# A hybrid decoder layer in one Trainium2 core: the short convolution's norm takes its power of 128x256 instead of 128x2

## The chip, the core and the metric

The kernel runs on one core of a Trainium2 chip. The metric is device time in microseconds. The median of three timed runs before the change is 1239.05 us (1238.25 to 1240.45). The engines of the core are named as in the profile: PE (TensorE, matmuls), PEld (its weight loads), DVE (VectorE), ACT (ScalarE), POOL (GpSimd), SP (SyncE, here the queue that issues the weight DMAs).

## The reference, cut to what matters

The layer is: RMSNorm, one input projection (`w_in`, 2048 to 6144), attention on 8 heads, a gated short convolution on the other 1024 columns, an output projection, cross-attention into 256 memory tokens, a SwiGLU FFN and a final RMSNorm, all for 256 tokens in float32. The change touches the norm of the convolution branch:

```
y_conv = b_gate * short_conv(c_gate * x_in, w_conv, b_conv)
y_conv = rms_norm(y_conv.reshape(bsz, s_len, CONV_GROUPS, HEAD_DIM), g_conv_out...)   # 8 groups of 128 columns
merged = jnp.concatenate([o_attn..., y_conv...], axis=-1);  return merged @ w_out
```

`rms_norm(x, g)` is `x * rsqrt(mean(x*x) + 1e-6) * g`, the mean here over the 128 columns of a group, for each token by itself.

## The kernel before, in words

All large products run over one stream of weights. A step `j` is one pair of 128-row weight tiles, 128x1024: a DMA of SP brings it into `raw`, ACT casts it to `whi` (L644), DVE forms the rest `wlo = raw - whi` (`split`, L937), and PE does 12 matmuls of 128x512 with it (`step`, L378 to L380: high by high, high by low, low by high, for two halves of the tokens). ACT and DVE run the cast and the split of step `j + 2` (`LEAD`) in their iteration `j`, and the ring has four places. There is no planner: the order on each engine is the order in the code, an iteration `j` after another, and semaphores hold an engine until its input is there. PE's step `j` waits for `lo_ready` (the split of step j).

The steps that matter here are 88 to 111. Steps 88 to 95 are the last group of the input projection (`G_X`), 96 to 103 the keys of the memory (`G_KX`), 104 to 111 the first group of the output projection (`G_OUT`). In iterations 94 to 101 ACT and DVE also prepare the memory's activations for steps 96 to 103 (`untransposed`, L680 on ACT, two instructions at L972 on DVE, signal `m_lo`). Steps 108 to 111 wait for `merged_conv`: step 111 for all eight blocks of the convolution.

The convolution is laid between the steps. It has 8 blocks `b` of 128 channels; block b starts at step s = 92 + 2b (`CONV_START`), and its channels lie on the partitions, its 256 tokens on the free axis. By iteration of each engine:

- s: PE transposes x and the gate into PSUM (L467), ACT forms two products of it (L778, L779), DVE adds the two other taps and the gate (`conv_taps`, L1089, L1092, L1094).
- s+1: ACT squares it into `csq` (L786).
- s+2: PE sums the squares over the partitions, 2 matmuls of 128x1 with `csq` as the weights (`conv_sums`, L475), so that the sums lie with tokens on the partitions, 128x2. DVE scales them and adds the epsilon (`conv_mean`, L1098). POOL takes the power -0.5 of 128x2 (L356).
- s+3: DVE writes the roots on two 128x128 diagonals, over `csq` (`conv_diagonal`, L1105).
- s+4: PE multiplies ones by these diagonals (`conv_spreading`, L482), so that each partition has the root of each token, and DVE scales y with it and the gain (`conv_scale`, L1112).
- s+5: ACT writes the high part (`conv_out`, L790), POOL the low part (L359, signal `merged_conv`).

POOL's order is: the product `u` of blocks 0 to 3 (L352, 128x1024), powers 0 and 1, the product of blocks 4 to 7 (L352 again), then low part 0, power 2, low part 1, power 3, and so on, so that the low part of b stands right behind the power of b + 1. On DVE, in one iteration, the order is `split`, `conv_taps`, `conv_mean`, `conv_diagonal`, `conv_scale`, `untransposed`.

Of the kernel before, what the change touches and what calls it, by code (L numbers as in the profile page):

```python
# [20 lines left out]
P = 128  # L21
# [72 lines left out]
def build(nc, stream, x, xT, mem, memT, params, pos, inv_freq, g_final, out):  # L94
# [4 lines left out]
    with ctx:  # L99
# [3 lines left out]
        def sb(name, shape, dt=f32, at=None):  # L103

            size = 4 * int(np.prod(shape[1:]))
            spot = place if at is None else at
            line = LINE if size >= LINE else 64
            where = -(-spot[0] // line) * line
            spot[0] = where + -(-size // 64) * 64
            return nc.alloc_sbuf_tensor_at(name, shape, dt, offset=where)  # L110
# [6 lines left out]
        def sem(name):  # L117
            return ctx.enter_context(nc.semaphore(name))
# [14 lines left out]
        rstd = sb("rstd", [P, 4, TT])  # L133
        vpe = sb("vpe", [P, 4, TT])
        part = sb("part", [P, TT, D // GC])
        cvar = sb("cvar", [P, CB, TT])
        crstd = sb("crstd", [P, CB, TT])
        fss = sb("fss", [P, TT])
        fvar = sb("fvar", [P, TT])
        frstd = sb("frstd", [P, TT])  # L140
# [23 lines left out]
        uT = sb("uT", [P, 2, 2 + SEQ], at=conv_at)  # L164
        cy = sb("cy", [P, 4, SEQ], at=conv_at)
        csq = sb("csq", [P, 4, SEQ], at=conv_at)
        place[0] = max(place[0], conv_at[0])
        assert place[0] <= nc.sbuf_usable_end, (place[0], nc.sbuf_usable_end)
        par_cols = G_KX * GC
# [68 lines left out]
        u_ready, conv_T, conv_u = sem("u_ready"), sem("conv_T"), sem("conv_u")  # L238
        conv_tap, conv_y, conv_sq = sem("conv_tap"), sem("conv_y"), sem("conv_sq")
        conv_ss, conv_var, conv_root = sem("conv_ss"), sem("conv_var"), sem("conv_root")  # L240
        conv_diag, conv_spread = sem("conv_diag"), sem("conv_spread")
        conv_norm, conv_hi, merged_conv = sem("conv_norm"), sem("conv_hi"), sem("merged_conv")
        pad_ready = sem("pad_ready")
        q2_T, q2T_ready = sem("q2_T"), [sem("q2T_by_act"), sem("q2T_by_dve")]
# [27 lines left out]
        def gain(col):  # L272
            return par[:, ds(col, 1)]
# [24 lines left out]
        @block.gpsimd  # L298
        def _(pool):
            pool.memset(ident[:], 0.0).then_inc(blank, 1)  # L300
            pool.memset(mask[:], 0.0).then_inc(blank, 1)
            pool.memset(ones[:], 1.0).then_inc(consts_ready, 1)
            pool.memset(mhalf[:], -0.5).then_inc(consts_ready, 1)
            pool.wait_ge(blank, 2)
            pool.affine_select(out=ident[:], in_=ident[:], compare_op=ALU.not_equal, fill=1.0, base=0,
                               pattern=[[-1, P]], channel_multiplier=1).then_inc(consts_ready, 1)
            for n in (0, 2):
                pool.affine_select(out=mask[:, n * P:(n + 1) * P], in_=mask[:, n * P:(n + 1) * P],
                                   compare_op=ALU.is_ge, fill=MASKED, base=0,
                                   pattern=[[-1, P]], channel_multiplier=1).then_inc(consts_ready, 1)  # L310

            def root(n):

                pool.wait_ge(var_ready, n + 1)
                nc.gpsimd.tensor_tensor(rstd[:, n, :], vpe[:, n, :], mhalf[:], ALU.pow).then_inc(rstd_ready, 1)

            def rope(h, parity):
                src = proj[:, :, ds(AW + h * (2 * HD), 2 * HD)].rearrange("p t (q f) -> p t q f", q=2)
                lo_half, hi_half = src[:, :, :, 0:HD // 2], src[:, :, :, HD // 2:HD]
                pool.wait_ge(rope_done, 2 * h)  # L320
                for n, (a, b) in enumerate(((lo_half, cos), (hi_half, sin), (hi_half, cos), (lo_half, sin))):
                    nc.gpsimd.tensor_tensor(rtmp[:, n], a, b[:], ALU.mult).then_inc(rope_products, 1)
                pool.wait_ge(rope_products, 4 * h + 4)
                dst = qkr[:, parity]
                nc.gpsimd.tensor_tensor(dst[:, :, :, 0:HD // 2], rtmp[:, 0], rtmp[:, 1], ALU.subtract).then_inc(rope_done, 1)
                nc.gpsimd.tensor_tensor(dst[:, :, :, HD // 2:HD], rtmp[:, 2], rtmp[:, 3], ALU.add).then_inc(rope_done, 1)

            def head_root(h):
                pool.wait_ge(o_var, h + 1)
                nc.gpsimd.tensor_tensor(orstd, ovar, mhalf[:], ALU.pow).then_inc(o_rstd, 1)  # L330

            pool.wait_ge(consts_ready, 2)
            root(0)
            root(1)
            pool.wait_ge(table_ready, 4)
            await_out(pool, G_QK)
            rope(0, 0)
            rope(1, 1)
            with pool.Fori(0, NH // 2 - 1) as i:
                for n in range(2):  # L340
                    h = i * 2 + n
                    head_root(h)

                    pool.wait_ge(qk_T, h + 1)
                    rope(h + 2, n)
            head_root(NH - 2)
            head_root(NH - 1)
            c0, x0 = (G_C - G_V) * GC, (G_X - G_V) * GC
            for n in range(2):
                await_out(pool, G_X + n)  # L350
                u = proj[:, :, x0 + n * GC:x0 + (n + 1) * GC]
                nc.gpsimd.tensor_tensor(u, proj[:, :, c0 + n * GC:c0 + (n + 1) * GC], u, ALU.mult).then_inc(u_ready, 1)  # L352
                for j in range((G_X + 1) * SPG, G_KX * SPG + 1) if n == 0 else range(G_KX * SPG + 1, G_XQ * SPG):
                    for b in conv_blocks(j, 2):
                        pool.wait_ge(conv_var, b + 1)
                        nc.gpsimd.tensor_tensor(crstd[:, b, :], cvar[:, b, :], mhalf[:], ALU.pow).then_inc(conv_root, 1)  # L356
                    for b in conv_blocks(j, 5):
                        pool.wait_ge(conv_hi, b + 1)
                        nc.gpsimd.tensor_tensor(alo[:, NH + b, :], cy[:, b % 4, :], ahi[:, NH + b, :].bitcast(f32),  # L359
                                                ALU.subtract).then_inc(merged_conv, 1)  # L360
            root(2)
            root(3)
            for t in range(TT):
                pool.wait_ge(fvar_ready, t + 1)
                nc.gpsimd.tensor_tensor(frstd[:, t:t + 1], fvar[:, t:t + 1], mhalf[:, 0:1], ALU.pow).then_inc(frstd_ready, 1)  # L365
# [3 lines left out]
        def _(pe):  # L369
# [101 lines left out]
            def conv_sums(b):  # L471

                pe.wait_ge(conv_sq, b + 1)
                for t in range(TT):
                    done = nc.tensor.matmul(ps[:, CONV_BANKS[b % 4], SEQ + t:SEQ + t + 1],  # L475
                                            lhsT=csq[:, b % 4, t * P:(t + 1) * P], rhs=ones[:, 0:1], start=True, stop=True)
                done.then_inc(conv_ss, 1)

            def conv_spreading(b):

                pe.wait_ge(conv_diag, b + 1)
                nc.tensor.matmul(ps[:, CONV_BANKS[b % 4], 0:SEQ], lhsT=ones[:], rhs=csq[:, b % 4, :],  # L482
                                 start=True, stop=True).then_inc(conv_spread, 1)

            def conv_beside(j):

                for b in conv_blocks(j, 4):
                    conv_spreading(b)
                for b in conv_blocks(j, 2):
                    conv_sums(b)  # L490
                for b in conv_blocks(j, 0):
                    conv_front(b)
# [141 lines left out]
        def _(act):  # L634
# [147 lines left out]
            def conv_square(b):  # L782
                act.wait_ge(conv_y, b + 1)
                if b >= 4:
                    act.wait_ge(conv_spread, b - 3)
                nc.scalar.activation(csq[:, b % 4, :], cy[:, b % 4, :], ACT.Square).then_inc(conv_sq, 1)  # L786

            def conv_out(b):
# [140 lines left out]
        def _(dve):  # L929
# [165 lines left out]

            def conv_mean(b):
                dve.wait_ge(conv_ss, b + 1)
                vec.tensor_scalar(cvar[:, b, :], ps[:, CONV_BANKS[b % 4], SEQ:SEQ + TT], 1.0 / HD, EPS,  # L1098
                                  ALU.mult, ALU.add).then_inc(conv_var, 1)

            def conv_diagonal(b):

                dve.wait_ge(conv_root, b + 1)
                for t in range(TT):
                    done = vec.tensor_scalar(csq[:, b % 4, t * P:(t + 1) * P], ident[:], crstd[:, b, t:t + 1], None, ALU.mult)  # L1105
                done.then_inc(conv_diag, 1)

            def conv_scale(b):

                y = cy[:, b % 4, :]  # L1110
                dve.wait_ge(conv_spread, b + 1)
                vec.scalar_tensor_tensor(y, y, gain(C_CONV + b), ps[:, CONV_BANKS[b % 4], 0:SEQ],  # L1112
                                         ALU.mult, ALU.mult).then_inc(conv_norm, 1)

            dve.wait_ge(scores_ready, NH)
# [15 lines left out]
            for j in range((G_X + 1) * SPG + 3, J_XO):  # L1131
# [5 lines left out]
                    conv_taps(b)  # L1137
                for b in conv_blocks(j, 2):
                    conv_mean(b)
                for b in conv_blocks(j, 3):  # L1140
                    conv_diagonal(b)
                for b in conv_blocks(j, 4):
                    conv_scale(b)
                u = j - (G_X + 1) * SPG - 6
# [158 lines left out]
```

## Time and profile before

| | before |
|---|---|
| median of 3 runs | 1239.05 us |
| profiled execution, its own time | 1238.83 us |
| its span (first to last instruction) | 1237.0 us |
| PE busy | 1220.4 us (99%) |
| DVE, ACT, POOL busy | 676.0, 593.5, 87.6 us |
| DMA | 234.36 MB, mean 189 GB/s |

A busy share says only that an engine had work in its pipeline. What a change is worth is read from the chain of waits and from the timeline of its stage: which instruction an engine was waiting for when it stood still. POOL is idle for most of the span, and DVE for nearly half of it.

### The profile page before, as it was taken

How to read it: one execution, taken by the hardware profiler on the slowest of the kernel's cores; microseconds unless marked ns; L12 is line 12 of the kernel's file. 1: busy time of each engine (PE TensorE's matmuls, PEld its weight loads, DVE VectorE, ACT ScalarE, POOL GpSimd, SP SyncE). 2: the span in 40 equal slices, each digit the busy share in tenths (PEclk: the TensorE clock that was granted, in tenths of full speed). 3: DMA queues.
4: the chain of work that ended last, by engine and by line, in shares of the span. 5: the costliest groups of instructions: out<-in, count | busy, mean ns of one | idle time of the engine just before them, and what ended most of it. 6: DMA issues, size and time to landing. Idle time of an engine off the chain costs nothing.

```text
span 1237.0 us, 16477 instructions
## 1 busy us (share of the span) xinstructions
PE 1220.4 (99%) x5564; PEld 1011.9 (82%) x5564; DVE 676.0 (55%) x804; ACT 593.5 (48%) x759; POOL 87.6 (7%) x91
## 2 busy tenths in 40 slices
PE   8999999999999999999999999999999999999997
PEld 7888888887888888888888888888888888888886
DVE  6655555557855676554554455455455454544543
ACT  6665554546644664644444444444444343444432
POOL 0042422212200000000000000000000000000000
PEclk9999999999999999999999999999999999999999
DMA  9755555555455544566555555555555565656562
GB/s 356 276 187 176 167 172 181 170 168 206 156 184 187 171 154 161 180 225 199 187 186 190 187 185 200 186 186 187 188 186 187 186 188 173 216 177 212 172 209 114
DMA packets 64830, 234.36 MB, mean 189 GB/s; under 512 B 7584, under 2 KB 7584, under 8 KB 64416
## 3 DMA queue, kind: packets, MB, share of 16 engines
q1 hardware_dynamic: 62784, 226.52, 54.7%
q10 hardware_dynamic: 2016, 7.43, 1.6%
q8 instruction: 20, 0.33, 0.1%
q14 instruction: 10, 0.08, 0.0%
HBM read 231.83 MB, written 2.10 MB: 189 GB/s over the span
## 4 chain that ended last, share of the span: by engine, by line
PE 96%; DVE 2%; ACT 1%; issue 1%; DMA 0%; POOLq 0%; POOL 0%; ACTq 0%
PE ps L378 31%; PE ps L380 31%; PE ps L379 31%; PE ps L402 1%; DVE wlo L937 1%; PE ps L467 0%; PE ps L482 0%; DMA stage<-x_T 0%; PE ps L422 0%; PE ps L427 0%; PE ps L549 0%; PE ps L475 0%; PE ps L433 0%; DVE small L1065 0%; PE ps L571 0%
## 5 line engine op out<-in xcount | busy, mean ns | idle before, releaser
L937 DVE TENSOR_TENSOR wlo<-raw,whi 128x1024 fp32r<-128x1024 f32 x424 | 523.1, 1235 | 438.5 <-ACT whi L644 434.7
L644 ACT ACTIVATE whi<-raw 128x1024 fp32r<-128x1024 f32 x424 | 448.6, 1059 | 460.5 <-PE ps L380 453.1
L378 PE MATMUL ps<-whi,ahi 128*128 128x512 f32 x864 | 339.7, 393 | 0.0
L380 PE MATMUL ps<-whi,alo 128*128 128x512 f32 x864 | 336.7, 390 | 0.0
L379 PE MATMUL ps<-wlo,ahi 128*128 128x512 f32 x864 | 336.3, 389 | 0.0
L380 PEld LDWEIGHTS ps<-whi,alo 128*128 128x128 f32 x864 | 162.2, 188 | 34.2
L379 PEld LDWEIGHTS ps<-wlo,ahi 128*128 128x128 f32 x864 | 162.3, 188 | 32.8
L378 PEld LDWEIGHTS ps<-whi,ahi 128*128 128x128 f32 x864 | 162.3, 188 | 32.7
L378 PE MATMUL ps<-whi,bhi 128*128 128x512 f32 x448 | 180.3, 402 | 2.2 <-DVE wlo L937 2.2
L380 PE MATMUL ps<-whi,blo 128*128 128x512 f32 x448 | 175.3, 391 | 0.0
L379 PE MATMUL ps<-wlo,bhi 128*128 128x512 f32 x448 | 174.7, 390 | 0.0
L378 PE MATMUL ps<-whi,fhi 128*128 128x512 f32 x352 | 137.0, 389 | 0.0
L380 PE MATMUL ps<-whi,flo 128*128 128x512 f32 x352 | 136.9, 389 | 0.0
L379 PE MATMUL ps<-wlo,fhi 128*128 128x512 f32 x352 | 136.9, 389 | 0.0
L378 PEld LDWEIGHTS ps<-whi,bhi 128*128 128x128 f32 x448 | 84.5, 189 | 18.5 <-issue 2.3
L380 PEld LDWEIGHTS ps<-whi,blo 128*128 128x128 f32 x448 | 84.2, 188 | 18.3
L379 PEld LDWEIGHTS ps<-wlo,bhi 128*128 128x128 f32 x448 | 84.5, 189 | 16.4
L380 PEld LDWEIGHTS ps<-whi,flo 128*128 128x128 f32 x352 | 66.1, 188 | 13.8
L378 PEld LDWEIGHTS ps<-whi,fhi 128*128 128x128 f32 x352 | 66.1, 188 | 13.7
L379 PEld LDWEIGHTS ps<-wlo,fhi 128*128 128x128 f32 x352 | 66.1, 188 | 13.5
L365 POOL TENSOR_TENSOR frstd<-fvar,mhalf 128x1 f32<-128x1 f32 x2 | 1.1, 550 | 718.4 <-DVE fvar L1257 718.4
L651 ACT ACTIVATE fhi<-ps 128x512 f32 (+1 forms) x22 | 13.0, 598 | 44.4 <-PE ps L402 44.4
(163 smaller groups left out, 614.9 us busy)
## 6 DMA issues: line engine op xcount, KB each, us to landing
raw<-w_stream SPq DMA_DIRECT2D x424, 512.0 KB, 3.3
stage<-x_T SPq DMA_DIRECT2D x8, 256.0 KB, 5.5
res<-x_in ACTq DMA_DIRECT2D x4, 512.0 KB, 7.6
stage<-mem_in ACTq DMA_DIRECT2D x4, 512.0 KB, 6.7
proj<-mem_T ACTq DMA_DIRECT2D x2, 1024.0 KB, 6.9
y_out<-yout SPq DMA_DIRECT2D x4, 512.0 KB, 3.0
gfin<-g_final ACTq DMA_DIRECT2D x1, 1024.0 KB, 8.1
par<-params ACTq DMA_DIRECT2D x1, 56.0 KB, 4.2
```

What stands on the lines that cost most here:

```text
L365: nc.gpsimd.tensor_tensor(frstd[:, t:t + 1], fvar[:, t:t + 1], mhalf[:, 0:1], ALU.pow).then_inc(frstd_ready, 1)
L378: nc.tensor.matmul(bank, lhsT=a_h, rhs=w_h, start=first and n == 0, stop=False)
L379: nc.tensor.matmul(bank, lhsT=a_h, rhs=w_l, start=False, stop=False)
L380: done = nc.tensor.matmul(bank, lhsT=a_l, rhs=w_h, start=False, stop=last and n == KS - 1)
L402: done = nc.tensor.transpose(bank[:, n, t * P:(t + 1) * P], src[:, t, (k + n) * P:(k + n + 1) * P], ident[:])
L644: nc.scalar.activation(tile_pair(whi, j), tile_pair(raw, j), ACT.Copy).then_inc(hi_ready, 1)
L651: done = nc.scalar.activation(hi[:, ds(uk + k, KS), :], bank, ACT.Copy)
L937: vec.tensor_tensor(tile_pair(wlo, j), tile_pair(raw, j), tile_pair(whi, j).bitcast(f32), ALU.subtract).then_inc(lo_ready, 1)
```

## The change

The sum over the partitions is taken by a matmul of `ones` (128x128) by `csq` (128x256), which leaves the sum of each token on every partition. The scaling with the epsilon is then done on 128x256 (from PSUM into `csq`), and POOL takes the power of 128x256, in place, against a tile `mhalves` of 128x256 that it fills once at the start. `conv_scale` reads the roots from `csq` in SBUF instead of from PSUM, and waits for POOL instead of for PE. The two diagonals on DVE and the spreading matmul on PE go, and so do `cvar` and `crstd`. ACT's square of block b waits for the scale of block b - 4 instead of its spreading.

```diff
--- before.py
+++ after.py
@@ -133,8 +133,6 @@
         rstd = sb("rstd", [P, 4, TT])
         vpe = sb("vpe", [P, 4, TT])
         part = sb("part", [P, TT, D // GC])
-        cvar = sb("cvar", [P, CB, TT])
-        crstd = sb("crstd", [P, CB, TT])
         fss = sb("fss", [P, TT])
         fvar = sb("fvar", [P, TT])
         frstd = sb("frstd", [P, TT])
@@ -164,6 +162,8 @@
         uT = sb("uT", [P, 2, 2 + SEQ], at=conv_at)
         cy = sb("cy", [P, 4, SEQ], at=conv_at)
         csq = sb("csq", [P, 4, SEQ], at=conv_at)
+        mhalves = sb("mhalves", [P, SEQ], at=conv_at)
+        assert conv_at[0] - 4 * SEQ >= place[0]
         place[0] = max(place[0], conv_at[0])
         assert place[0] <= nc.sbuf_usable_end, (place[0], nc.sbuf_usable_end)
         par_cols = G_KX * GC
@@ -238,7 +238,7 @@
         u_ready, conv_T, conv_u = sem("u_ready"), sem("conv_T"), sem("conv_u")
         conv_tap, conv_y, conv_sq = sem("conv_tap"), sem("conv_y"), sem("conv_sq")
         conv_ss, conv_var, conv_root = sem("conv_ss"), sem("conv_var"), sem("conv_root")
-        conv_diag, conv_spread = sem("conv_diag"), sem("conv_spread")
+        halves_ready = sem("halves_ready")
         conv_norm, conv_hi, merged_conv = sem("conv_norm"), sem("conv_hi"), sem("merged_conv")
         pad_ready = sem("pad_ready")
         q2_T, q2T_ready = sem("q2_T"), [sem("q2T_by_act"), sem("q2T_by_dve")]
@@ -301,6 +301,7 @@
             pool.memset(mask[:], 0.0).then_inc(blank, 1)
             pool.memset(ones[:], 1.0).then_inc(consts_ready, 1)
             pool.memset(mhalf[:], -0.5).then_inc(consts_ready, 1)
+            pool.memset(mhalves[:], -0.5).then_inc(halves_ready, 1)
             pool.wait_ge(blank, 2)
             pool.affine_select(out=ident[:], in_=ident[:], compare_op=ALU.not_equal, fill=1.0, base=0,
                                pattern=[[-1, P]], channel_multiplier=1).then_inc(consts_ready, 1)
@@ -346,6 +347,7 @@
             head_root(NH - 2)
             head_root(NH - 1)
             c0, x0 = (G_C - G_V) * GC, (G_X - G_V) * GC
+            pool.wait_ge(halves_ready, 1)
             for n in range(2):
                 await_out(pool, G_X + n)
                 u = proj[:, :, x0 + n * GC:x0 + (n + 1) * GC]
@@ -353,7 +355,7 @@
                 for j in range((G_X + 1) * SPG, G_KX * SPG + 1) if n == 0 else range(G_KX * SPG + 1, G_XQ * SPG):
                     for b in conv_blocks(j, 2):
                         pool.wait_ge(conv_var, b + 1)
-                        nc.gpsimd.tensor_tensor(crstd[:, b, :], cvar[:, b, :], mhalf[:], ALU.pow).then_inc(conv_root, 1)
+                        nc.gpsimd.tensor_tensor(csq[:, b % 4, :], csq[:, b % 4, :], mhalves[:], ALU.pow).then_inc(conv_root, 1)
                     for b in conv_blocks(j, 5):
                         pool.wait_ge(conv_hi, b + 1)
                         nc.gpsimd.tensor_tensor(alo[:, NH + b, :], cy[:, b % 4, :], ahi[:, NH + b, :].bitcast(f32),
@@ -471,21 +473,11 @@
             def conv_sums(b):
 
                 pe.wait_ge(conv_sq, b + 1)
-                for t in range(TT):
-                    done = nc.tensor.matmul(ps[:, CONV_BANKS[b % 4], SEQ + t:SEQ + t + 1],
-                                            lhsT=csq[:, b % 4, t * P:(t + 1) * P], rhs=ones[:, 0:1], start=True, stop=True)
-                done.then_inc(conv_ss, 1)
-
-            def conv_spreading(b):
-
-                pe.wait_ge(conv_diag, b + 1)
                 nc.tensor.matmul(ps[:, CONV_BANKS[b % 4], 0:SEQ], lhsT=ones[:], rhs=csq[:, b % 4, :],
-                                 start=True, stop=True).then_inc(conv_spread, 1)
+                                 start=True, stop=True).then_inc(conv_ss, 1)
 
             def conv_beside(j):
 
-                for b in conv_blocks(j, 4):
-                    conv_spreading(b)
                 for b in conv_blocks(j, 2):
                     conv_sums(b)
                 for b in conv_blocks(j, 0):
@@ -782,7 +774,7 @@
             def conv_square(b):
                 act.wait_ge(conv_y, b + 1)
                 if b >= 4:
-                    act.wait_ge(conv_spread, b - 3)
+                    act.wait_ge(conv_norm, b - 3)
                 nc.scalar.activation(csq[:, b % 4, :], cy[:, b % 4, :], ACT.Square).then_inc(conv_sq, 1)
 
             def conv_out(b):
@@ -1095,21 +1087,14 @@
 
             def conv_mean(b):
                 dve.wait_ge(conv_ss, b + 1)
-                vec.tensor_scalar(cvar[:, b, :], ps[:, CONV_BANKS[b % 4], SEQ:SEQ + TT], 1.0 / HD, EPS,
+                vec.tensor_scalar(csq[:, b % 4, :], ps[:, CONV_BANKS[b % 4], 0:SEQ], 1.0 / HD, EPS,
                                   ALU.mult, ALU.add).then_inc(conv_var, 1)
 
-            def conv_diagonal(b):
-
+            def conv_scale(b):
+
+                y = cy[:, b % 4, :]
                 dve.wait_ge(conv_root, b + 1)
-                for t in range(TT):
-                    done = vec.tensor_scalar(csq[:, b % 4, t * P:(t + 1) * P], ident[:], crstd[:, b, t:t + 1], None, ALU.mult)
-                done.then_inc(conv_diag, 1)
-
-            def conv_scale(b):
-
-                y = cy[:, b % 4, :]
-                dve.wait_ge(conv_spread, b + 1)
-                vec.scalar_tensor_tensor(y, y, gain(C_CONV + b), ps[:, CONV_BANKS[b % 4], 0:SEQ],
+                vec.scalar_tensor_tensor(y, y, gain(C_CONV + b), csq[:, b % 4, :],
                                          ALU.mult, ALU.mult).then_inc(conv_norm, 1)
 
             dve.wait_ge(scores_ready, NH)
@@ -1137,8 +1122,6 @@
                     conv_taps(b)
                 for b in conv_blocks(j, 2):
                     conv_mean(b)
-                for b in conv_blocks(j, 3):
-                    conv_diagonal(b)
                 for b in conv_blocks(j, 4):
                     conv_scale(b)
                 u = j - (G_X + 1) * SPG - 6
```

## Rows read from the trace of the kernel before

**Rows 1.** The page: span, busy time of PE, chain that ended last, by engine.
```profile
span 1237.0 us, 16477 instructions
PE 1220.4 (99%) x5564; PEld 1011.9 (82%) x5564; DVE 676.0 (55%) x804; ACT 593.5 (48%) x759; POOL 87.6 (7%) x91
...
PE 96%; DVE 2%; ACT 1%; issue 1%; DMA 0%; POOLq 0%; POOL 0%; ACTq 0%
```

**Rows 2.** Waits of 280 to 350 us: us in total, times, longest us.
```profile
POOL crstd L356 <- DVE cvar L1098: 49.8, 8, 15.9
```

**Rows 3.** Groups of POOL by shape: busy us, mean ns of one, idle before.
```profile
L356 POOL TENSOR_TENSOR crstd<-cvar,mhalf 128x2 f32<-128x2 f32 x8 | 5.7, 710 | 49.8 <-DVE cvar L1098 49.8
L330 POOL TENSOR_TENSOR small<-small,mhalf 128x2 f32<-128x2 f32 x8 | 5.6, 700 | 135.4 <-DVE small L1062 135.4
...
L365 POOL TENSOR_TENSOR frstd<-fvar,mhalf 128x1 f32<-128x1 f32 x2 | 1.1, 550 | 718.4 <-DVE fvar L1257 718.4
```

**Rows 4.** Tile views of crstd and alo: duration ns least/median/most, starts, shape.
```profile
L356 POOL TENSOR_TENSOR crstd<-cvar,mhalf x8: 688/689/860, 289.9 to 339.2; 128x2 f32<-128x2 f32 x8
...
L359 POOL TENSOR_TENSOR alo<-cy,ahi x8: 857/1206/1702, 300.0 to 346.0; 128x256 fp32r<-128x256 f32 x8
```

**Rows 5.** Timeline, blocks 0 to 2: start us, us, instruction, idle before it.
```profile
289.94 0.86 POOL L356 TENSOR_TENSOR crstd<-cvar,mhalf 128x2 f32<-128x2 f32 x1 [15.92 <-DVE cvar L1098]
...
296.69 0.69 POOL L356 TENSOR_TENSOR crstd<-cvar,mhalf 128x2 f32<-128x2 f32 x1 [5.89 <-DVE cvar L1098]
...
296.92 0.87 DVE L972 SCALAR_TENSOR_TENSOR blo<-proj,par,bhi 128x256 fp32r<-128x256 f32 x2
...
297.35 2.69 POOL L352 TENSOR_TENSOR proj<-proj 128x1024 f32<-128x1024 f32 x1
...
297.71 3.42 DVE L937 TENSOR_TENSOR wlo<-raw,whi 128x1024 fp32r<-128x1024 f32 x1
...
302.04 0.92 PE L482 MATMUL ps<-csq,ones 128*128 128x256 f32 x2 [2.40 <-DVE csq L1105]
...
305.47 0.48 DVE L1089 SCALAR_TENSOR_TENSOR cy<-uT,par,cy 128x256 f32<-128x256 f32 x1 [1.56 <-ACT cy L779]
...
306.51 0.42 DVE L1094 TENSOR_TENSOR cy<-ps,cy 128x256 f32<-128x256 f32 x1
306.85 0.15 DVE L1098 TENSOR_SCALAR cvar<-ps 128x2 f32<-128x2 f32 x1
```

**Rows 6.** Timeline of DVE, block 5: two splits with the diagonals between them.
```profile
321.96 1.22 DVE L937 TENSOR_TENSOR wlo<-raw,whi 128x1024 fp32r<-128x1024 f32 x1
323.10 0.97 DVE L1105 TENSOR_SCALAR csq<-ident,crstd 128x128 f32<-128x128 f32 x2
```

**Rows 7.** Timeline, block 7 and the start of step 111.
```profile
344.96 0.48 DVE L1112 SCALAR_TENSOR_TENSOR cy<-cy,par,ps 128x256 f32<-128x256 f32 x1 [0.78 <-PE ps L482]
...
345.55 0.40 ACT L790 ACTIVATE ahi<-cy 128x256 fp32r<-128x256 f32 x1
...
346.03 1.47 POOL L359 TENSOR_TENSOR alo<-cy,ahi 128x256 fp32r<-128x256 f32 x1 [4.80 <-ACT ahi L790]
...
347.53 1.03 PE L512 MATMUL ps<-ident,proj 128*128 128x128 f32 x8
348.32 0.48 PE L378 MATMUL ps<-whi,ahi 128*128 128x512 f32 x1
```

**Rows 8.** Pieces of the chain at 302 to 306 us: start us, us, what.
```profile
293.34 0.34 PE ps L475 x4
...
304.99 0.43 PE ps L379
...
306.80 0.23 PE ps L379
```

**Rows 9.** One stretch: us, busy us of PE, PEld, DVE, ACT, POOL; granted clock.
```profile
302.00:306.00 4.00, 3.96 (x15) 3.51 (x16) 2.40 (x5) 1.40 (x4) 0.00 (x0) 0.57 0.61 204
```

**Rows 10.** Timeline of the start: POOL's fills, PE's warming matmuls, its first step.
```profile
0.88 0.42 POOL L301 MEMSET mask<- 128x384 f32 x1
...
9.38 0.47 PE L378 MATMUL ps<-whi,bhi 128*128 128x512 f32 x1 [2.17 <-DVE wlo L937]
```

More of the change, by code:

```diff
@@ L1097, in conv_mean @@
                 dve.wait_ge(conv_ss, b + 1)
-                vec.tensor_scalar(cvar[:, b, :], ps[:, CONV_BANKS[b % 4], SEQ:SEQ + TT], 1.0 / HD, EPS,
+                vec.tensor_scalar(csq[:, b % 4, :], ps[:, CONV_BANKS[b % 4], 0:SEQ], 1.0 / HD, EPS,
                                   ALU.mult, ALU.add).then_inc(conv_var, 1)
-            def conv_diagonal(b):
-                dve.wait_ge(conv_root, b + 1)
-                for t in range(TT):
-                    done = vec.tensor_scalar(csq[:, b % 4, t * P:(t + 1) * P], ident[:], crstd[:, b, t:t + 1], None, ALU.mult)
-                done.then_inc(conv_diag, 1)
             def conv_scale(b):
                 y = cy[:, b % 4, :]
-                dve.wait_ge(conv_spread, b + 1)
-                vec.scalar_tensor_tensor(y, y, gain(C_CONV + b), ps[:, CONV_BANKS[b % 4], 0:SEQ],
+                dve.wait_ge(conv_root, b + 1)
+                vec.scalar_tensor_tensor(y, y, gain(C_CONV + b), csq[:, b % 4, :],
                                          ALU.mult, ALU.mult).then_inc(conv_norm, 1)
```

## The prediction

> **What bounds the kernel now.** I read the page first, then the waits of the stretch in which the convolution runs, then the timeline of that stretch. The page says that PE is busy for 99% of the span and makes up 96% of the chain that ended last [rows 1]. So time can be gained only by taking work from PE, or where PE stands still; it can be lost wherever an engine that feeds PE falls behind by more than its lead of two to three steps. The whole change lies between 280 and 350 us. There POOL is the idlest engine: in front of its eight powers it waited 49.8 us in total for DVE's scaled sums [rows 2]. PE itself stood still once for long, 2.40 us at 302.04 [rows 5]. The chain of that stall starts on POOL. Its product L352 of 128x1024 ran from 297.35 to 300.04, and DVE's split, started at 297.71, took 3.42 us [rows 5] where one takes 1.22 [rows 6]: the split did not advance while POOL read its two operands. The diagonals came late, and with them L482 on PE. Two things matter for what follows: a two-operand instruction of POOL can stop a two-operand instruction of DVE, and DVE's order is fixed, so whatever stops DVE stops the splits.
>
> **What goes.** PE's two column sums cost 0.34 us of its chain per block [rows 8], 8 x 0.34 = 2.7 us. The new ones matmul at that place is the spreading matmul of before, with the same shape, and the old one goes, so nothing is added. On DVE the two diagonals go: 0.97 us per block [rows 6], 8 x 0.97 = 7.8 us, of an engine that is not the bound. The stall of 2.40 us goes in its present form. PE's clock fell after it: 0.57 granted from 302 to 306 us [rows 9], with 0.43 us between matmuls where 0.23 is usual [rows 8], which cost about 3.8 x (1 - 0.23/0.43) = 1.8 us.
>
> **What is added on DVE.** The scaling and epsilon reads 128x256 from PSUM instead of 128x2. The nearest row is L1094, which reads 128x256 from PSUM: 0.42 us busy and 0.34 us to the start of the next instruction, against 0.15 of L1098 [rows 5]. That is 0.3 us per block, less than the diagonals free. The scale L1112 reads its roots from SBUF; L972, with two SBUF operands of 128x256, takes 0.87 us for two [rows 5], so 0.44 to 0.48 each, as now. No cost.
>
> **What is added at the start.** One fill of 128x256 by POOL. The fill of 128x384 took 0.42 us [rows 10], so at most 0.42. It moves PE's warming matmuls by that much, but PE's first step had 2.17 us of idle before it, waiting for DVE's split [rows 10]. Hidden.
>
> **What is added on POOL: the power of 128x256.** This decides the case. No power of that shape runs in the trace. There are two shapes: 128x1 in 550 ns and 128x2 in 700 and 710 ns on average [rows 3], at the least 688, median 689 [rows 4]. The difference is 139 ns for one more element per partition. A plain subtraction of 128x256 takes 857 ns at the least [rows 4], and L352 2.69 us for 1024, which is 2.6 ns per element [rows 5]. So the power is not like the other operations: it costs fifty times as much per element, as if it were worked out by a long routine for one element of each partition after another. From below, it costs what the subtraction costs plus the start-up that the power of 128x1 shows, 0.86 + 0.55 = 1.4 us. By the slope, it is 0.55 + 255 x 0.139 = 36.0 us. From above, if there were no fixed part at all, 256/2 x 0.69 = 88 us. I take 36.0, since it is the only difference between two measured sizes of this very operation.
>
> The Trainium skill (GPSIMD Engine Reference, Elementwise — side-by-side cycle accounting) gives about 2.6 cycles per element for GpSimd's elementwise operations at 1.2 GHz, which would be an estimate of 0.6 us for 256 elements; by it the change would come out near 1233 us, as in the second rival. That page measured an add. The subtraction's row is near it and the rows of the power are not. The same page (Performance pitfalls for Q7 kernels) says that a dependent chain of fp32 operations costs 4 cycles a link, and by it 139 ns would be a chain of some forty links.
>
> **What a power of 36 us does.** A block comes every two steps, which at 12 matmuls x 0.23 us is 5.5 us. Eight powers on one engine cannot keep up. DVE's scale L1112 of block b waits for the power of b, and behind it in DVE's order are `untransposed` and the splits of steps s+7 onwards, so PE stops. Besides, there is the effect seen at 297.71: while POOL reads operands for 36 us, DVE's two-operand instructions (L972, L937) don't advance. The short power at 296.69 did not hold up the L972 at 296.92 [rows 5], but it had only two elements to read; the long one reads until near its end, as L352 does. I take this as the likelier case and walk through it.
>
> Power 0 starts at 289.94 now [rows 5]. With 0.3 us for the longer scaling and a short wait for an L972 it starts at about 290.5. After each power DVE has to do, before the next scaled sum is there: two pairs of L972 (0.79 from start to start, the 296.92 to the 297.71 in [rows 5]), two splits (323.10 - 321.96 = 1.13 each [rows 6]), the taps (306.85 - 305.47 = 1.38 [rows 5]) and the scaling (0.34). That is 2 x 0.79 + 2 x 1.13 + 1.38 + 0.34 = 5.6 us while L972 runs (iterations 94 to 101, the gaps behind powers 0 to 3), and 4.0 us behind powers 4 to 6. POOL puts its low part in each gap from the second on (0.9 us), and L352 behind power 1 (2.7 us). The gaps are then 5.6, 9.2, 6.5, 6.5, 4.9, 4.9 and 4.9, together 42.5 us. PE's two steps per block, even at 0.43 us per matmul 10.3 us, lie beside the next power. ACT's casts and copies do too. Power 7 ends at 290.5 + 8 x 36.0 + 42.5 = 621.0.
>
> Behind it: low part 6 (0.9), two splits (2.3), the scale (0.48), ACT's high part (0.40) and the low part 7 (0.86), 5.1 us with 0.1 for the hand-overs: 626.1. PE's step 111 waits for that. It starts now at 348.32, just behind the last low part, which ends at 346.03 + 1.47 = 347.50 [rows 7]. So the end moves by 626.1 - 348.3 = 277.8 us, and by 1.8 for the clock after the last stall, as after the one at 302. What goes on PE (2.7 us) lies before step 111, beside the powers, and brings nothing. The profiled execution took 1238.83 us, 0.2 us below the median of the runs: 1238.8 + 279.6 = **1518 us**. If the 710 ns of the average is taken instead of 689, the slope is 160 ns, a power 41.4 us and the time 1561.
>
> **Rivals.**
>
> *The powers don't hold DVE up* (no lock for the whole power). Then the scaled sum of b + 1, which stands ahead of the scale of b in DVE's order, is ready when power b ends, and powers run back to back with only POOL's own work between: 290.2 + 8 x 36.0 + 2.7 + 6 x 0.9 = 586.3, then 0.9 + 0.48 + 0.40 + 0.86 + 0.1 = 589.0. The end moves by 240.7 and 1.8: 1481 us. For it speaks the L972 at 296.92, which ran through a short power; against it the 3.42 us split. In the trace L972 would then be short during a power.
>
> *The power is cheap at this width.* This is the one on the other side, faster. If the 139 ns are the price of a slow path for odd elements and a wide power streams like a subtraction, it takes 1.4 us. Then PE loses 2.7 us of work, the stall of 2.40 and up to 1.8 of clock, some of it given back to the powers that now stop the splits: 1238.8 - 2.7 - 3 = 1233 us. It decides from where power and low part fit beside a block with DVE's share: DVE has about 1 us free of diagonals, so up to about 2 us per power it is faster or even, and above that slower. For it speaks only that two narrow shapes say little of a wide one; against it, that three lines of the same operation give the same slope.
>
> *The routine works on several elements at once in a wide power.* One power then costs, say, a quarter per element, 35 ns or 9.4 us. With the same gaps power 7 ends at 290.5 + 75.2 + 42.5 = 408.2, the low part at 413.3, the end moves by 65.0 + 1.8: 1306 us. A power of 6 us gives about 1280.
>
> **How the numbers follow.** 36 us with the hold-up has 0.46, 36 us without it 0.22, between 3 and 30 us per power 0.14, a steeper power 0.03, a power of 1.4 to 2 us 0.12 and no difference 0.03. The likeliest case is 1518, with its own range 1495 to 1565. The range of 8 in 10 must take in the second and most of the third: 1280 to 1565. Within 0.2% (2.5 us), which is about what a measurement of this kernel can tell from no change, 0.03; faster 0.12; slower 0.85.
>
> **What would show it.** Right: L356 at 128x256 near 36 us eight times; PE at rest for some 30 us in front of each pair of steps between 293 and 625 us; one L972 or L937 in each gap as long as a power; outside that stretch the same profile. Wrong: a power of under 2 us; powers back to back, with DVE waiting at L1112 instead of stretched; low parts that don't set step 111.

## The result, and the profile after

The changed kernel takes 1523.49 us (median of 4 runs, 1523.21 to 1523.79) against 1239.75 us for the kernel before in the same comparison. The ratio is 1.2295 (95% interval 1.228 to 1.2309): 23% slower. The forecast was 1518 us.

The page of the kernel after, with the slices (each a fortieth of the span, in tenths), the chain by engine and line, and the costliest group of POOL:

```profile
span 1521.4 us, 16399 instructions
...
PE 1235.5 (81%) x5532; PEld 1020.2 (67%) x5532; DVE 679.1 (45%) x788; ACT 592.8 (39%) x759; POOL 409.2 (27%) x92
...
PE   8999999821122211499999999999999999999997
...
POOL 0052230499999999500000000000000000000000
PEclk9999999955565555699999999999999999999999
...
PE 75%; POOL 22%; DVE 1%; ACT 1%; issue 0%; DMA 0%; POOLq 0%; ACTq 0%
PE ps L380 24%; PE ps L382 24%; PE ps L381 24%; POOL csq L358 22%; PE ps L404 1%; POOL alo L361 0%; DMA stage<-x_T 0%; PE ps L424 0%; PE ps L429 0%; PE ps L541 0%; PE ps L435 0%; DVE wlo L929 0%; POOL proj L354 0%; DVE small L1057 0%; PE ps L563 0%
...
L358 POOL TENSOR_TENSOR csq<-csq,mhalves 128x256 f32<-128x256 f32 x8 | 331.1, 41387 | 16.2 <-DVE csq L1090 16.2
```

One line of POOL, eight instructions, is now 22% of the chain, where POOL had 0% of it before [rows 1]. In the slices POOL is full for a stretch of 340 us and PE works a tenth to a quarter of it. POOL's wait for the scaled sums, 49.8 us before [rows 2], is 16.2, and that all in front of the first power: since then POOL has always had the next one waiting. The timeline of POOL there:

```profile
290.29 82.62 POOL L358 TENSOR_TENSOR csq<-csq,mhalves 128x256 f32<-128x256 f32 x2 [16.21 <-DVE csq L1090]
372.88 2.34 POOL L354 TENSOR_TENSOR proj<-proj 128x1024 f32<-128x1024 f32 x1
375.18 0.92 POOL L361 TENSOR_TENSOR alo<-cy,ahi 128x256 fp32r<-128x256 f32 x1
376.06 41.41 POOL L358 TENSOR_TENSOR csq<-csq,mhalves 128x256 f32<-128x256 f32 x1
...
586.36 41.41 POOL L358 TENSOR_TENSOR csq<-csq,mhalves 128x256 f32<-128x256 f32 x1
627.74 0.72 POOL L361 TENSOR_TENSOR alo<-cy,ahi 128x256 fp32r<-128x256 f32 x1
629.27 1.19 POOL L361 TENSOR_TENSOR alo<-cy,ahi 128x256 fp32r<-128x256 f32 x1 [0.81 <-ACT ahi L782]
```

Powers stand one behind another, with only low parts and the one product between. What DVE does beside them (timeline of DVE, from the first power on):

```profile
290.12 1.36 DVE L964 SCALAR_TENSOR_TENSOR blo<-proj,par,bhi 128x256 fp32r<-128x256 f32 x2
291.40 1.21 DVE L929 TENSOR_TENSOR wlo<-raw,whi 128x1024 fp32r<-128x1024 f32 x1
292.54 0.87 DVE L964 SCALAR_TENSOR_TENSOR blo<-proj,par,bhi 128x256 fp32r<-128x256 f32 x2
293.33 1.21 DVE L929 TENSOR_TENSOR wlo<-raw,whi 128x1024 fp32r<-128x1024 f32 x1
...
296.15 0.41 DVE L1090 TENSOR_SCALAR csq<-ps 128x256 f32<-128x256 f32 x1
331.75 0.94 DVE L1097 SCALAR_TENSOR_TENSOR cy<-cy,par,csq 128x256 f32<-128x256 f32 x1 [35.19 <-POOL csq L358]
```

Power 0 runs from 290.29 to 331.7 us (the first row above holds powers 0 and 1), and DVE's splits inside it take 1.21 us, as always. DVE stops only at 296.6, at the scale that needs the power's result. So a power does not hold DVE's two-operand instructions up for its length. It does so for about half a microsecond at its start (timeline of both engines, narrow windows behind the start of powers 0 and 4):

```profile
290.51 0.97 DVE L964 SCALAR_TENSOR_TENSOR blo<-proj,par,bhi 128x256 fp32r<-128x256 f32 x1
...
460.18 41.40 POOL L358 TENSOR_TENSOR csq<-csq,mhalves 128x256 f32<-128x256 f32 x1
...
460.42 1.74 DVE L929 TENSOR_TENSOR wlo<-raw,whi 128x1024 fp32r<-128x1024 f32 x1
```

The L964 takes 0.97 us instead of 0.48 and the split 1.74 us instead of 1.21. It is so behind each of the eight powers: DVE's first two-operand instruction to start behind the power's start, within 0.25 us of it, is 0.46 to 0.53 us longer than its kind, and those that follow it are not. The step that closes the stretch:

```profile
630.52 0.80 PE L380 MATMUL ps<-whi,ahi 128*128 128x512 f32 x1 [38.18 <-POOL alo L361]
631.11 0.63 PE L381 MATMUL ps<-wlo,ahi 128*128 128x512 f32 x1
```

It is PE's step 111, and it waits for the last low part, as the prediction had it. It started at 348.32 before [rows 7]: 282.2 us later, of 284.4 us that the profiled executions differ by (1523.21 - 1238.83).

### The profile page after: what moved, and what is told of

Read it like the earlier page. It is cut to its first block, busy times and chain, and to the rows that moved or that the text cites. A ratio compares the mean times of both kernels' runs of the same rounds, so it can differ in the third digit from the quotient of the medians.

```text
span 1521.4 us, 16399 instructions
## 1 busy us (share of the span) xinstructions
PE 1235.5 (81%) x5532; PEld 1020.2 (67%) x5532; DVE 679.1 (45%) x788; ACT 592.8 (39%) x759; POOL 409.2 (27%) x92
## 4 chain that ended last, share of the span: by engine, by line
PE 75%; POOL 22%; DVE 1%; ACT 1%; issue 0%; DMA 0%; POOLq 0%; ACTq 0%
PE ps L380 24%; PE ps L382 24%; PE ps L381 24%; POOL csq L358 22%; PE ps L404 1%; POOL alo L361 0%; DMA stage<-x_T 0%; PE ps L424 0%; PE ps L429 0%; PE ps L541 0%; PE ps L435 0%; DVE wlo L929 0%; POOL proj L354 0%; DVE small L1057 0%; PE ps L563 0%
## 5 line engine op out<-in xcount | busy, mean ns | idle before, releaser
L929 DVE TENSOR_TENSOR wlo<-raw,whi 128x1024 fp32r<-128x1024 f32 x424 | 521.7, 1233 | 434.6 <-ACT whi L636 430.8
L380 PE MATMUL ps<-whi,ahi 128*128 128x512 f32 x864 | 344.8, 399 | 171.7 <-DVE wlo L929 98.1
L382 PE MATMUL ps<-whi,alo 128*128 128x512 f32 x864 | 340.3, 394 | 0.0
L381 PE MATMUL ps<-wlo,ahi 128*128 128x512 f32 x864 | 340.3, 394 | 0.0
L358 POOL TENSOR_TENSOR csq<-csq,mhalves 128x256 f32<-128x256 f32 x8 | 331.1, 41387 | 16.2 <-DVE csq L1090 16.2
L1097 DVE SCALAR_TENSOR_TENSOR cy<-cy,par,csq 128x256 f32<-128x256 f32 x8 | 9.1, 1142 | 289.4 <-POOL csq L358 289.4
L782 ACT ACTIVATE ahi<-cy 128x256 fp32r<-128x256 f32 x8 | 3.3, 416 | 299.2 <-DVE cy L1097 299.2
```

What stands on the lines that cost most here:

```text
L358: nc.gpsimd.tensor_tensor(csq[:, b % 4, :], csq[:, b % 4, :], mhalves[:], ALU.pow).then_inc(conv_root, 1)
L380: nc.tensor.matmul(bank, lhsT=a_h, rhs=w_h, start=first and n == 0, stop=False)
L381: nc.tensor.matmul(bank, lhsT=a_h, rhs=w_l, start=False, stop=False)
L382: done = nc.tensor.matmul(bank, lhsT=a_l, rhs=w_h, start=False, stop=last and n == KS - 1)
L782: nc.scalar.activation(ahi[:, NH + b, :], cy[:, b % 4, :], ACT.Copy).then_inc(conv_hi, 1)
L929: vec.tensor_tensor(tile_pair(wlo, j), tile_pair(raw, j), tile_pair(whi, j).bitcast(f32), ALU.subtract).then_inc(lo_ready, 1)
```

## The experiments

Each ratio is to the kernel before in the same comparison, which took 1238.8 us in all of them. Code is cut to the lines that matter.

**1. A ladder of powers where nobody waits for them.** The kernel before with this behind POOL's fourth root, beside the FFN:

```diff
+            pool.memset(lab_a[:], 1.7).then_inc(lab, 1)
+            pool.memset(lab_b[:], -0.5).then_inc(lab, 1)
+            ladder = [(P, n, ALU.pow) for n in (1, 2, 4, 16, 64, 256)]
+            ladder += [(64, 256, ALU.pow), (16, 256, ALU.pow), (P, 256, ALU.mult)]
+            for n, (rows, cols, op) in enumerate(ladder):
+                pool.wait_ge(lab, n + 2)
+                nc.gpsimd.tensor_tensor(lab_a[0:rows, 0:cols], ..., lab_b[0:rows, 0:cols], op).then_inc(lab, 1)
```

> The kernel before, with a ladder of powers on POOL behind its fourth root, where POOL is idle until the end and nobody waits for them: 128 partitions by 1, 2, 4, 16, 64 and 256, then 64x256 and 16x256, then a product of 128x256, each waiting for the last. Theory A (a price per element of the free axis, whatever the partitions): 0.39 us + 0.160 us per element, so 0.55, 0.71, 1.03, 2.95, 10.6 and 41.4 us, and 41.4 us also for 64x256 and 16x256; the product 0.73 us. Theory B (a price per element in all): 64x256 at 20.9 us, 16x256 at 5.5 us. On the hold-up: if the long power doesn't hold up DVE, the splits beside it keep 1.23 us and the time stays at 1239 to 1240 us; if it held them, each power of 256 elements would stop PE for over 30 us and the time would be near 1340 us.

Measured: 1238.4 us, ratio 0.9999 (0.999 to 1.0009). Groups of POOL by shape (busy, mean ns):

```profile
L374 POOL TENSOR_TENSOR lab_a<-lab_a,lab_b 16x256 f32<-16x256 f32 x1 | 42.3, 42258 | 0.1
L374 POOL TENSOR_TENSOR lab_a<-lab_a,lab_b 64x256 f32<-64x256 f32 x1 | 41.6, 41621 | 0.1
...
L374 POOL TENSOR_TENSOR lab_a<-lab_a,lab_b 128x64 f32<-128x64 f32 x1 | 10.5, 10548 | 0.1
...
L374 POOL TENSOR_TENSOR lab_a<-lab_a,lab_b 128x16 f32<-128x16 f32 x1 | 3.0, 2977 | 0.1
...
L374 POOL TENSOR_TENSOR lab_a<-lab_a,lab_b 128x4 f32<-128x4 f32 x1 | 1.0, 1007 | 0.1
L374 POOL TENSOR_TENSOR lab_a<-lab_a,lab_b 128x2 f32<-128x2 f32 x1 | 0.7, 703 | 0.1
L374 POOL TENSOR_TENSOR lab_a<-lab_a,lab_b 128x1 f32<-128x1 f32 x1 | 0.6, 552 | 0.1
```

In the timeline of that stretch the power of 128x256 is 41.25 us, and the product of the same shape 0.735. From 4 to 256 elements the price is (41.25 - 1.01)/252 = 0.160 us for each element of the free axis, from 1 to 2 it is 0.151. 64 or 16 partitions cost as much as 128. Theory A holds, B falls. And the splits beside the ladder (tile view of wlo, 515 to 655 us; the ladder runs from 514 to 656) keep their length:

```profile
L949 DVE TENSOR_TENSOR wlo<-raw,whi x51: 1224/1226/1227, 515.7 to 654.5; 128x1024 fp32r<-128x1024 f32 x51
```

None of them started in the first half microsecond of a wide power, so the hold at the start could not show on DVE here. It shows on POOL. The powers of 64x256 and 16x256 started at 571.70 and 613.40, while these two splits ran:

```profile
571.00 1.23 DVE L949 TENSOR_TENSOR wlo<-raw,whi 128x1024 fp32r<-128x1024 f32 x1 [0.92 <-ACT whi L656]
...
613.34 1.23 DVE L949 TENSOR_TENSOR wlo<-raw,whi 128x1024 fp32r<-128x1024 f32 x1 [2.07 <-ACT whi L656]
```

The splits still had 0.53 and 1.17 us to run, and the powers took 0.37 and 1.01 us longer than the 41.25 of 128x256, which met no split at its start beyond 0.14 us. This fits a power that waits for a running split and then starts.

**2. A product in place of the power.** The change with all its parts but the price of the power.

```diff
-                        nc.gpsimd.tensor_tensor(csq[:, b % 4, :], csq[:, b % 4, :], mhalves[:], ALU.pow)...
+                        nc.gpsimd.tensor_tensor(csq[:, b % 4, :], csq[:, b % 4, :], mhalves[:], ALU.mult)...
```

> The kernel after, with a product in place of POOL's power of 128x256, so its roots are wrong and all else stays. If the power's duration is the whole loss, this is the change without it: 2.7 us less on PE, the diagonals gone, the stall at 302 us shorter or gone: 1231 to 1237 us. If part of the loss lies elsewhere (the wider scaling on DVE, the scale that now has two operands in SBUF, the longer hops), it stays above 1241 us.

Measured: 1232.98 us (1232.78 to 1233.08), ratio 0.9954 (0.9937 to 0.9971). The rest of the change makes the kernel faster by 5.8 us; the whole loss is the duration of the power. This kernel leaves out the root, as experiment 5 does; experiments 3 and 9 take it of some columns only.

**3. The power of 64 columns.** The kernel after with `csq[:, b % 4, 0:64]` and `mhalves[:, 0:64]` at the same line.

> The kernel after, with the power taken of the first 64 columns only, so the other roots are wrong. A power should take 0.39 + 64 x 0.160 = 10.6 us. Theory A (POOL's powers back to back, DVE not held up): power 7 ends at 290.3 + 8 x 10.6 + 2.3 + 6 x 0.7 = 381.6, step 111 starts 2.8 us later at 384.4, 36 us later than before: 1239 + 36 + 2 = 1277 us. Theory B of the prediction (hold-up, gaps of 42.5 us between powers): 1239 + 36 + 35 + 2 = 1312 us.

Measured: 1277.66 us, ratio 1.0313 (1.0295 to 1.033); a power takes 10.72 us in the timeline, and powers are back to back. Theory A was within 1 us, the hold-up is 34 us off. The hold at the start is there again, and shorter (timelines of POOL and DVE, power 4 and the split behind its start):

```profile
337.25 10.73 POOL L358 TENSOR_TENSOR csq<-csq,mhalves 128x64 f32<-128x64 f32 x1
...
337.50 1.34 DVE L929 TENSOR_TENSOR wlo<-raw,whi 128x1024 fp32r<-128x1024 f32 x1
```

**4. The root by ACT and DVE.** The kernel after with POOL out of the norm (the comments name the iteration).

```diff
+                nc.scalar.activation(csq[:, b % 4, :], cy[:, b % 4, :], ACT.Square, scale=HD ** -0.5)   # s+1
+                nc.scalar.activation(csq[:, b % 4, :], ps[:, CONV_BANKS[b % 4], 0:SEQ], ACT.Sqrt, bias=eps[:])   # s+3
+                vec.reciprocal(csq[:, b % 4, :], csq[:, b % 4, :])   # s+4, then the scale
```

> The kernel after, with the power taken off POOL: ACT squares with the scale 1/sqrt(128), takes the square root of the spread sum from PSUM with the epsilon as its bias (128x256, at s+3), DVE takes the reciprocal of 128x256 in front of its scale at s+4. By the theory that only the power's duration cost time, this is as fast as the product in its place: 1231 to 1237 us, if a reciprocal of 128x256 takes under 1 us on DVE. Rival: the reciprocal is long too, or the table for the square root is loaded again and again between the other functions (1.28 us each, 8 times or more), and it ends at 1240 us or above.

Measured: 1242.24 us, ratio 1.0032 (1.0021 to 1.0044): the rival. Groups of 280 to 355 us:

```profile
L1094 DVE RECIPROCAL csq<-csq 128x256 f32<-128x256 f32 x8 | 13.9, 1742 | 0.0
...
L777 ACT ACT_TABLE_LOAD x1 | 1.3, 1283 | 0.0
```

The table is loaded once in this stretch; the reciprocal is not under 1 us but 1.74, 13.9 us of DVE in all. PE then waits for DVE's L966, which prepares the memory behind it, and step 111 for the last low part (waits, 280 to 360 us):

```profile
PE ps L375 <- DVE blo L966: 4.1, 3, 1.4
...
PE ps L375 <- POOL alo L356: 3.7, 1, 3.7
```

These 7.8 us are most of the 9.3 us by which this kernel is slower than experiment 2.

**5. Fifty-six products in place of each power.** The kernel after. Does only the length on POOL count?

```diff
-                        nc.gpsimd.tensor_tensor(csq[...], csq[...], mhalves[:], ALU.pow).then_inc(conv_root, 1)
+                        for n_p in range(56):
+                            pool.wait_ge(lab, 55 * b + n_p)
+                            done = nc.gpsimd.tensor_tensor(lab_a[:] if n_p < 55 else csq[...], csq[...], mhalves[:], ALU.mult)
```

> The kernel after, with 56 products of 128x256 in place of each power, each behind the last, so its roots are wrong: about the same length on POOL (56 x 0.73 = 41 us against 41.4), but made of instructions that stream two operands. Theory A (only the length counts): 1523 us as with the power. Theory B (a product and a two-operand instruction of DVE keep each other out, a power doesn't): DVE's splits and L964 beside the products show 1.7 to 1.9 us where they show 1.21 beside a power, and POOL waits in its turn, so a block gets longer by what DVE's two-operand work of a block lasts, about 5 us: 1523 + 8 x 5 = 1563 us, 1545 at the least.

Measured: 1567.08 us, ratio 1.2649 (1.2629 to 1.2669). A block's products last 47.1 us, where a power lasts 41.4: theory B by the total. Not all of the 5.7 us are turns with DVE, though. Where DVE stands still, 46 products follow one another every 0.80 us:

```profile
299.72 36.83 POOL L364 TENSOR_TENSOR lab_a<-csq,mhalves 128x256 f32<-128x256 f32 x46
```

The expectation reckoned with 0.73 us for each and left out the hand-over from one to the next. At 0.80 a block has 56 x 0.80 = 44.9 us; only the other 2.2 us are turns with DVE, where theory B had about 5. So that its 1563 us came so near is partly luck. What shows the turns themselves are DVE's splits. Tile view of wlo, first the kernel after (286 to 632 us):

```profile
L929 DVE TENSOR_TENSOR wlo<-raw,whi x19: 1209/1214/1747, 285.1 to 631.1; 128x1024 fp32r<-128x1024 f32 x19
```

and then the kernel with the products (286 to 670 us):

```profile
L938 DVE TENSOR_TENSOR wlo<-raw,whi x17: 1226/1748/1759, 285.2 to 627.8; 128x1024 fp32r<-128x1024 f32 x17
```

The median split takes 1.75 us beside products and 1.21 beside powers. Products and two-operand work of DVE take turns all the time. A power takes part in that only at its start: the 1747 in the first line is one of the four splits that stand behind the start of powers 4 to 7.

**6. The product of blocks 4 to 7 in four pieces, in the kernel before.**

```diff
-                nc.gpsimd.tensor_tensor(u, proj[:, :, c0 + n * GC:c0 + (n + 1) * GC], u, ALU.mult).then_inc(u_ready, 1)
+                for q in range(4 if n else 1):   # pieces of 128 columns for n = 1
+                    done = nc.gpsimd.tensor_tensor(u[:, :, q * w:(q + 1) * w], ..., u[:, :, q * w:(q + 1) * w], ALU.mult)
+                done.then_inc(u_ready, 1)
```

> The kernel before, with the product of blocks 4 to 7 on POOL (128x1024, 2.69 us) cut in four of 128x256. If the stall of PE at 302 us comes from one split that waits for the whole product, the split and the diagonals are through earlier, PE's wait of 2.40 us and the clock's 1.8 us go: 1235 to 1237 us. If DVE is held as long in sum by four pieces, it stays at 1239 us.

Measured: 1237.01 us, ratio 0.9988 (0.9979 to 0.9997). PE's wait of 2.40 us for the diagonals [rows 5] becomes 1.24:

```profile
297.85 1.76 DVE L941 TENSOR_TENSOR wlo<-raw,whi 128x1024 fp32r<-128x1024 f32 x1
...
301.02 0.70 PE L486 MATMUL ps<-csq,ones 128*128 128x256 f32 x2 [1.24 <-DVE csq L1109]
```

The split is through in 1.76 us instead of 3.42, but the next instructions of DVE wait for the next pieces: the two diagonals take 1.43 us, where they take 0.97 undisturbed [rows 6]. The granted clock is 1.00 from 302 to 306 us, where it was 0.57 [rows 9]. The time is 1.8 us shorter, somewhat under half of the 4.2 us that stall and clock together would give.

**7. The narrow power, and the column of roots as PE's weights.** The kernel before without its diagonals:

```diff
-                pe.wait_ge(conv_diag, b + 1)
-                nc.tensor.matmul(ps[:, CONV_BANKS[b % 4], 0:SEQ], lhsT=ones[:], rhs=csq[:, b % 4, :],
+                pe.wait_ge(conv_root, b + 1)
+                for t in range(TT):
+                    done = nc.tensor.matmul(ps[:, CONV_BANKS[b % 4], t * P:(t + 1) * P],
+                                            lhsT=crstd[:, b, t:t + 1].to_broadcast([P, P]), rhs=ident[:],
                                 start=True, stop=True)
```

> The kernel before, with the narrow power kept and the two diagonals gone another way: PE takes the column of roots, repeated 128 times as its weights, by the identity, two matmuls of 128x128, which leaves each token's root on every partition. DVE is rid of 7.8 us, PE's two matmuls should cost 0.25 us (half of the four transposes' 0.50) where the spreading costs 0.43, and the wait for the diagonals at 302 us goes: 1238.8 - 8 x 0.18 - 2.4 - 1.8 = 1233 us. If the stall comes back in another wait, 1237 us.

Measured: 1234.25 us (1233.86 to 1234.31), ratio 0.9963 (0.9949 to 0.9977). It computes the whole layer and is 4.6 us faster than the kernel before. PE no longer waits: the chain has its two matmuls at 299.67, behind the last of a step, while the split still takes 3.42 us (timeline, then a piece of the chain):

```profile
297.74 3.42 DVE L940 TENSOR_TENSOR wlo<-raw,whi 128x1024 fp32r<-128x1024 f32 x1
```

```profile
299.67 0.44 PE ps L483 x4
```

The two matmuls cost 0.44 us, not 0.25, as much as the one they replace. The gain is the stall and the clock behind it alone (the granted clock is 1.00 from 302 to 306 us): 1238.8 - 2.4 - 1.8 = 1234.6.

**8. Both together.**

> Both edits together: the repeated root as weights, and the product in four pieces. If the stall at 302 us had one cause, it is gone with either, and this is as fast as the repeated root alone: 1233 us. If what holds up the split still costs something without the diagonals, it is up to 2 us faster than that.

Measured: 1234.3 us, ratio 0.9963 (0.9949 to 0.9977). With the diagonals gone, the pieces bring nothing more. Both work on one cause, the wait for the diagonals: this way it is gone, with the pieces alone (experiment 6) it was only shortened.

**9. The power of 24 columns.** As the third experiment, with 24.

> The kernel after, with the power taken of the first 24 columns only, so the other roots are wrong. A power should take 0.39 + 24 x 0.160 = 4.2 us. POOL's share of a block is then 4.2 + 0.9 = 5.1 us against the 5.5 us of two steps. Theory: POOL limits only when its share of a block exceeds two steps, so this is as fast as the product in the power's place, 1233 us, at most 1237 us for the low parts that DVE stretches. Rival: the hop from the scaled sum through POOL to DVE's scale is on the path at any length, and 8 x 3.3 us more per power cost 1245 us or above.

Measured: 1231.16 us (1231.09 to 1231.28), ratio 0.9936 (0.9919 to 0.9952). Two groups of 286 to 350 us:

```profile
L358 POOL TENSOR_TENSOR csq<-csq,mhalves 128x24 f32<-128x24 f32 x8 | 34.7, 4336 | 22.1 <-DVE csq L1090 22.0
L929 DVE TENSOR_TENSOR wlo<-raw,whi 128x1024 fp32r<-128x1024 f32 x21 | 25.8, 1227 | 4.8 <-ACT whi L636 4.7
```

A power of 4.3 us costs the kernel nothing. The kernel is even 1.8 us faster than with the product of 0.91 us of experiment 2, where the same split took 1.43 us on average and PE waited 1.3 us for L964:

```profile
L929 DVE TENSOR_TENSOR wlo<-raw,whi 128x1024 fp32r<-128x1024 f32 x20 | 28.4, 1433 | 5.9 <-ACT whi L636 5.9
```

The two differ in width too, 24 columns against 256, and the width is what counts for DVE. Power 4 and the split behind its start (timelines of POOL and DVE):

```profile
317.77 4.33 POOL L358 TENSOR_TENSOR csq<-csq,mhalves 128x24 f32<-128x24 f32 x1 [1.15 <-DVE csq L1090]
...
318.00 1.26 DVE L929 TENSOR_TENSOR wlo<-raw,whi 128x1024 fp32r<-128x1024 f32 x1
```

The same place in three kernels, with an undisturbed split at 1.21 us:

| width of the power | its length | split behind its start | held by |
|---|---|---|---|
| 24 (experiment 9) | 4.3 us | 1.26 us | 0.05 us |
| 64 (experiment 3) | 10.7 us | 1.34 us | 0.13 us |
| 256 (kernel after) | 41.4 us | 1.74 us | 0.53 us |

The hold is about 2 ns for each column, near the 2.6 ns that the product L352 takes for one [rows 5], and a power's whole length is 160 ns for each. A split behind the start of a product of 128x256 takes 1.76 us (experiment 2, at 319.56 us), so a power and a product of one width hold it for about as long; the power only goes on for 40 us after that.

## Why the prediction was right

The sign, the place and the mechanism at large were right: eight wide powers on POOL outlast the two steps that a block has, DVE waits at the scale, the splits stand behind it, and the last low part sets step 111. Experiments 2, 3 and 9 show that the power's length does it: 0.9, 4.3, 10.7 and 41.4 us per power give 1233.0, 1231.2, 1277.7 and 1523.5 us. But that 1518 lies so close to 1523 is luck: two wrong steps, of 43 and 36 us, nearly cancel. Term by term, predicted and read from the trace after:

| term | predicted | measured | difference |
|---|---|---|---|
| start of power 0 | 290.5 | 290.29 | -0.2 |
| eight powers | 8 x 36.0 = 288.0 | 331.1 | +43.1 |
| what stands between them | 42.5 | 6.4 | -36.1 |
| from power 7 to step 111 | 5.1 | 2.75 | -2.4 |
| step 111 starts at | 626.1 | 630.5 | +4.4 |
| the rest: clock behind the stall | 1.8 | 2.2 (284.4 - 282.2) | +0.4 |

- *The price of a power.* The term was mis-sized, 36.0 us for 41.4. The step that failed is the slope: one difference between neighbouring sizes, 689 - 550 = 139 ns, was carried 255 times. The ladder has 552 and 703 ns, a step of 151 ns, and 0.160 us per element further up. Of the missing 5.4 us some 3 come from the first step (12 ns times 255) and some 2 from the dearer elements behind it. The average of 710 ns [rows 3] would have given 0.160 and the right 41.4 us, but by chance: seven of the eight powers took about 689 ns, one took 860 [rows 4], and that one makes the average, (7 x 689 + 860)/8 = 710. The bounds of 1.4 and 88 us, and the rival of a routine that speeds up when wide, fell with experiment 1.
- *The hold-up.* "The long one reads until near its end, as L352 does" was wrong, and with it the likelier of the two cases with a long power. It was taken from L352, a product; the runs show a hold of about 0.5 us at the start of a power of 41.4. The L972 at 296.92 that ran through a power [rows 5] spoke for the rival, but could not decide it: that a narrow power has little to read, as the prediction said against it, agrees with the hold of 0.05, 0.13 and 0.53 us for 24, 64 and 256 columns. The first rival is what happened, but for that half microsecond, and a sign that the prediction gave for being wrong came: powers back to back, with DVE waiting at its scale. With its own formula and the measured 41.4 us this rival gives 290.2 + 331.2 + 8.1 + 2.7 = 632.2 for step 111 and 1238.8 + 283.9 + 1.8 = 1524.5 us: 1.0 us from the measured time.
- *The tail.* The two splits ahead of the scale in the prediction were done during the power, since nothing held them for long; only scale, high part and low part remain. (The terms that the prediction names for the tail add up to 5.0 us, not 5.1.)
- *The small terms.* The scaling of 128x256 takes 0.41 us (0.42 foreseen). The rival's 1233 us for a cheap power was borne out by experiment 2. Its bound, about 2 us per power, was too low for a narrow power: 4.3 us is still faster. That bound was again built on a hold for the power's whole length.

What stays open is what a power does behind its first half microsecond. That the hold is in proportion to the width, and near the price of a product's columns, suggests that it takes in its operands at the start and then works on them without SBUF; the traces show the hold and its size, not the reading itself.

## What to carry to other kernels

Price an operation that is slow for each element by its cost per element of the free axis, with at least two sizes far apart; if only neighbouring sizes are at hand, carry the spread of their difference through, since it is multiplied, and don't trust an average that one long instruction makes. Such an operation belongs on the narrowest form of the data, and what has to be spread is cheaper spread behind it: a column repeated as the weights of a matmul by the identity does it without any other engine. How long an engine holds another up depends on the operation and on its width, and need not be the instruction's length. Look at the first instruction behind the start as well as at those in the middle.

## What the runs showed of the hardware

- POOL's power costs 0.39 us and 0.160 us per element of the free axis, for 16, 64 or 128 partitions alike (41.25 to 42.26 us for 256); a product of 128x256 takes 0.735 us, a power 56 times as long.
- A power holds DVE's two-operand instructions at its start only: 0.05, 0.13 and 0.53 us for 24, 64 and 256 columns, of 4.3, 10.7 and 41.4 us. Beside 140 us of powers, with no split starting right behind the start of a wide one, 51 splits took 1224 to 1227 ns. Products one behind another stretched the median split from 1.21 to 1.75 us.
- DVE's reciprocal of 128x256 from SBUF to SBUF takes 1.74 us, where the scale behind it, two products in one instruction (L1096), takes 0.48.
- A column of 128x1, repeated 128 times by a stride of zero, works as a weight tile on PE; two such f32 matmuls of 128x128 cost 0.44 us in the chain (experiment 7).
